# Slice by slice or tile by tile: the out-projection's end, its norm and the first FFN slice in another order

## The chip, the cores and the metric

The kernel runs on one core of a Trainium2 chip. The core has TensorE (PE in the rows; its weight loads are PEld), VectorE (DVE), ScalarE (ACT), GpSimd (POOL) and SyncE (SP), which issues nearly all loads. The metric is the device time of one execution, in microseconds (us), as the median of three runs.

## The reference, cut to what matters

The program is two transformer blocks in a row, 256 tokens by 1024 channels, in 32-bit floats. The first has attention and 32 experts. The second ends like this:

```python
mix = jnp.concatenate([attn, lru], axis=-1) @ w_out[l].astype(h.dtype)   # 1024 x 1024
x = x + rms_norm(mix, g_post_mix[l])
h = rms_norm(x, g_pre_ffn[l])
up = causal_dwconv(h @ w_up[l].astype(h.dtype), w_conv_ffn[l], b_conv_ffn[l])   # 1024 x 5632
c_u, c_g = jnp.split(up, 2, axis=-1)
ffn = (jax.nn.gelu(c_g, approximate=True) * c_u) @ w_down[l].astype(h.dtype)
x = x + rms_norm(ffn, g_post_ffn[l])
```

The change concerns the end of the product with `w_out`, the two norms behind it, and the first 256 columns of the product with `w_up`.

## The kernel before

**Split numbers.** A product keeps its precision by splitting both factors into an upper and a lower part, each of type fp32r, and adding three products: upper by upper, upper by lower, lower by upper (`mm3`). ScalarE writes the upper part as a rounded copy, VectorE the lower part as the difference. Weights are cut into slices of 128 x 2048 numbers, `s` counting them through the program. `split(s)` stands once in ScalarE's list (L768) and once in VectorE's (L1237). The parts go into `W`, which has two buffers, `s % 2`; `pair_free[s]` says when TensorE has read slice `s`, and `split(s)` on ScalarE waits for `pair_free[s - 2]`. The activations' parts are `X[:, 0]` and `X[:, 1]`, together `xin`.

**Order.** Each engine has its own list of instructions, written out by hand, and runs it in order; semaphores join them. The 256 tokens are two tiles `t` of 128. Weights come through a ring of eight places, loaded by SyncE in order; a place is loaded again once its slice is split (`lo_done`).

**Out-projection.** Slices 30 to 33 hold `w_out`, two blocks `k` of 128 rows each. For each `k`, tile and half `n` of the output columns, three matmuls over 512 columns add into a bank of PSUM `U_mix[t][n]`; so a slice is 24 matmuls. `rows_in` goes through slices 30, 31 and 32 with both tiles under each `k`. Only slice 33 goes tile by tile.

**Norms.** Of each finished half bank ScalarE takes the sum of squares (`square_rows`, L1152), then the root (`root_rows`, L786). VectorE multiplies by the gain (`gained`, L1857), takes the reciprocal (L1257) and adds to the residual `h` (`add_rows`, L1866). For the second norm ScalarE squares `h` (`square_h`, L1160) and takes the root; then the row is scaled into `u`: tile 0 by ScalarE (L1169), tile 1 by VectorE (L1885).

**Turns.** TensorE turns each tile, eight blocks of 128 x 128 (L2601), into banks `U_fT[t][0..1]`, four each. ScalarE rounds them with the gain into `X[:, 0]` (L1180), VectorE writes the remainder into `X[:, 1]` (L1896).

**FFN.** Slices 34 to 55 are `w_up`, 256 output columns each: 2 halves `m` x 8 `k` x 3 products = 48 matmuls, with the weights stationary and all 256 tokens moving. Slice 34 goes in `columns_first` (L2036): all upper by upper, then lower weights, then lower activations. The others go through `columns_in` (L1952). Slices 56 to 66 are `w_down`.

Of the kernel before, what the change touches and what calls it, by code (L numbers as in the profile page):

```python
# [8 lines left out]
F32 = mybir.dt.float32  # L9
# [7 lines left out]
P = 128  # L17
T = 256
# [96 lines left out]
def build_program(nc, I, out):  # L115
    ctx = ExitStack()
    with ctx:
        def sb(name, shape, dt=F32):
            return ctx.enter_context(nc.sbuf_tensor(name, shape, dt))

        def sem(name):
            return ctx.enter_context(nc.semaphore(name))
# [6 lines left out]
        h = sb("h", [P, 2, D])  # L129
        arena = sb("arena", [P, 20480])  # L130
# [267 lines left out]
        squares = Events(sem("s_squares"), attn=2, c=4, sb=2, mla=2, moe=2, ple=2, fin=4, mix=4, ffn=2, end=4)  # L398
        means = Events(sem("s_means"), fin=1)
        s_half = Events(sem("s_half_means"), mix=2, end=2)  # L400
        roots = Events(sem("s_roots"), attn=1, c=2, sb=1, mla=1, moe=2, ple=1, fin=2, mix=2, ffn=2, end=2)
        s_kT = sem("s_k_scaled")
        normed = Events(sem("s_normed"), attn=1, c=1, sb=1, mla=1, gates=1, fin=1, ffn=1)
# [32 lines left out]
        s_xfree, s_r0, s_u0 = sem("s_x_free"), sem("s_ffn_root0"), sem("s_ffn_rows0")  # L436
# [127 lines left out]

        def unloaded(n):
            if n in order:
                return lo_done(order[n])
            return BK.filled(U_pp[1][1]) if n == L_pp else used_at[n]
# [4 lines left out]
        def halved(s):  # L573
            n, b = SPL[s], s % 2
            w = loads[n][0]
            m = w.shape[1]
            return [W[:, b, j, 0:m * w.shape[2]].rearrange("p (a b) -> p a b", a=m) for j in range(2)]
# [177 lines left out]
        def _(e):  # L755
# [7 lines left out]
            def split(s):  # L763
                n = SPL[s]
                if s >= 2:
                    e.wait_ge(*pair_free[s - 2])
                e.wait_ge(s_land[loads[n][2]], 16 * loads[n][4])
                e.activation(halved(s)[0], loads[n][0], ACT.Copy).then_inc(s_hi, 1)  # L768
# [20 lines left out]
            def half_mean(name, t):  # L789
                e.wait_ge(*squares[name, 2 * t])  # L790
                e.activation(halfc[:, t:t + 1], ss[:, 2 * t:2 * t + 1], ACT.Identity, scale=1.0 / D,
                             bias=epsc).then_inc(s_half.sem, 1)

            def root_rows(name, t):
                e.wait_ge(*s_half[name, t])
                root(1, t, D, squares[name, 2 * t + 1], ss[:, 2 * t + 1:2 * t + 2], halfc[:, t:t + 1])
# [348 lines left out]
            split(33)  # L1145
            prime(ACT.Sqrt)
            split(34)
# [13 lines left out]

            square_rows("mix", 0, U_mix)
            root_rows("mix", 0)
            square_rows("mix", 1, U_mix)
            root_rows("mix", 1)
            square_h(0)
            root(1, 2, D, squares["ffn", 0], ss[:, 0:1])
            e.wait_ge(s_r0, 1)
            e.activation(u[:, 0, :], h[:, 0, :], ACT.Copy, scale=rs[:, 2:3]).then_inc(s_u0, 1)  # L1169
            square_h(1)  # L1170
            root(1, 3, D, squares["ffn", 1], ss[:, 1:2])

            for t in range(2):
                for i in range(2):
                    x = U_fT[t][i]
                    e.wait_ge(*BK.filled(x))
                    for j in range(4):
                        k = 4 * i + j
                        y = e.activation(X[:, 0, k, t * P:(t + 1) * P], ps[:, x[0], j * P:(j + 1) * P], ACT.Copy,  # L1180
                                         scale=col("g_pre_ffn_2", k))
                    y.then_inc(x_hi.sem, 1)
            split(35)
            prime(ACT.Gelu_apprx_tanh)
# [43 lines left out]
        def _(e):  # L1228
# [623 lines left out]
            split(33)  # L1852

            def gained(name, t, n, uses, gb):
                c = slice(n * 512, (n + 1) * 512)
                e.wait_ge(*squares[name, 2 * t + n])
                step(e.tensor_tensor(u[:, t, c], whole(uses[t][n]), gb[:, c], ALU.mult))  # L1857
# [13 lines left out]
            gained_rows("mix", 0, U_mix, gmix)  # L1871
            over_root("mix", 0, 0, 1)
            for n in range(2):
                add_rows(0, n, U_mix)
            gained_rows("mix", 1, U_mix, gmix)
            over_root("mix", 1, 1, 1)
            add_rows(1, 0, U_mix)
            e.wait_ge(*roots["ffn", 0])
            e.reciprocal(rs[:, 2:3], rs[:, 2:3]).then_inc(s_r0, 1)
            add_rows(1, 1, U_mix)  # L1880
            hi, lo = halved(34)
            e.wait_ge(s_hi, 35)
            e.tensor_tensor(lo[:, 0:4], loads[SPL[34]][0][:, 0:4], hi[:, 0:4].bitcast(F32), ALU.subtract)
            over_root("ffn", 1, 3, 1)
            e.tensor_scalar(u[:, 1, :], h[:, 1, :], rs[:, 3:4], None, ALU.mult).then_inc(normed.sem, 1)  # L1885
            e.tensor_tensor(lo[:, 4:8], loads[SPL[34]][0][:, 4:8], hi[:, 4:8].bitcast(F32), ALU.subtract).then_inc(s_lo, 1)

            for t in range(2):
# [46 lines left out]
            for t in range(2):  # L1936
                gained_rows("end", t, U_dd, gffn)
                over_root("end", t, t, 1)
                for n in range(2):
                    add_rows(t, n, U_dd)  # L1940
# [3 lines left out]
        def _(e):  # L1944
# [647 lines left out]
            for t in range(2):  # L2592
                if t == 0:
                    e.wait_ge(s_u0, 1)
                else:
                    e.wait_ge(*normed["ffn", 0])
# [6 lines left out]
            fT_ready = lambda k: [BK.emptied(U_fT[t][k // 4]) for t in range(2)]  # L2603
            fT_hi_ready = lambda k: [x_hi["ffn", 2 + k // 4]]
            for i in range(22):
                if i == 0:
                    columns_first(34, U_cv[0:2], range(KD), fT_hi_ready, fT_ready)
                    continue
# [55 lines left out]
```

## Time and profile before

| | us |
|---|---|
| median of 3 runs | 1410.53 |
| lowest, highest | 1408.81, 1411.22 |
| span of the profiled execution, first to last instruction | 1408.3 |
| its own total | not recorded apart from the span |
| TensorE busy in it | 1286.9 (91%) |
| TensorE's mean granted clock | 0.986 of full |

A profile is one execution; its times count from the first instruction. Busy times of several engines overlap, so shares don't add up to the span. A matmul's recorded duration includes its way through the array, which overlaps the next matmul: what one costs in a row is the distance from start to start. What ended a wait is inferred from semaphores. The granted clock is given as a share of 2.4 GHz: 1.00 is 2.4 GHz and 0.50 is 1.2 GHz.

### The profile page before, as it was taken

Reading aid. Unit: us, or ns where it says so; the run is one execution under the profiler, and the core shown is the slowest. Engines: PE = TensorE matmul, PEld = TensorE weight load, DVE = VectorE, ACT = ScalarE, POOL = GpSimd, SP = SyncE. Lnnn points to the kernel's source line nnn. Section 1 sums busy time; section 2 is a strip of 40 time slices with the busy share of each in tenths; the row PEclk is TensorE's granted clock in tenths of the full one; section 3 lists DMA queues with packets and bytes.
Section 4 is the critical chain, followed back from the end, with each engine's and each line's share of the span. In section 5 each row is a group of like instructions: output and inputs, shape, how many; then the busy total and the mean of one; then the engine's idle time right before and its main releaser. Section 6 shows DMA issues by size and latency. Waiting matters only on the chain.

```text
span 1408.3 us, 16583 instructions
## 1 busy us (share of the span) xinstructions
PE 1286.9 (91%) x6969; PEld 737.3 (52%) x6969; DVE 486.8 (35%) x730; ACT 401.2 (28%) x643; POOL 59.1 (4%) x115
## 2 busy tenths in 40 slices
PE   8999999999999889998888988889888999899998
PEld 7888433343333333333333332333324898799986
DVE  5895312112111111111211111111114687677765
ACT  5684212100110001100001000010004766655554
POOL 4001000000000000000000000000000510000000
PEclk9999899999999999999999999999999999899999
DMA  9548699999999999999999999999999964355520
GB/s 337 165 148 307 259 393 429 428 427 427 426 428 427 429 428 426 429 426 427 428 427 428 428 428 427 428 427 428 426 429 370 245 213 150 121 184 186 188 100 30
DMA packets 78474, 480.79 MB, mean 341 GB/s; under 512 B 5504, under 2 KB 40475, under 8 KB 53568
## 3 DMA queue, kind: packets, MB, share of 16 engines
q1 hardware_dynamic: 75904, 474.76, 83.3%
q0 software_dynamic: 2496, 4.96, 1.7%
q8 instruction: 57, 0.93, 0.3%
q14 instruction: 17, 0.14, 0.0%
HBM read 478.39 MB, written 1.31 MB: 341 GB/s over the span
## 4 chain that ended last, share of the span: by engine, by line
PE 52%; DMA 38%; DVE 4%; ACT 3%; issue 1%; DVEq 0%; ACTq 0%
DMA arena<-in_w_dn_dram 38%; PE ps L1952 22%; PE ps L2357 11%; PE ps L2397 11%; PE ps L2324 1%; PE ps L2413 1%; DVE W L1237 1%; PE ps L2036 1%; PE ps L1960 1%; PE ps L2514 1%; PE ps L2287 1%; ACT arena L960 0%; ACT arena L910 0%; PE ps L2368 0%; ACT W L768 0%
## 5 line engine op out<-in xcount | busy, mean ns | idle before, releaser
L2357 PE MATMUL ps<-ring,arena 128*64 128x512 f32 x1392 | 316.5, 597 | 12.0 <-DMA ring<-in_w_gu_dram 12.0
L2357 PEld LDWEIGHTS ps<-ring,arena 128*64 128x64 f32 x1392 | 97.4, 137 | 210.1 <-issue 179.1
L1952 PE MATMUL ps<-X,W 128*128 128x256 f32 x1560 | 191.4, 286 | 2.2 <-DVE W L1243 1.9
L1952 PEld LDWEIGHTS ps<-X,W 128*128 128x128 f32 x1560 | 190.2, 194 | 3.3 <-DVE W L1243 2.3
L1588 DVE TENSOR_SCALAR arena<-ps 128x512 f32<-128x512 f32 x32 | 22.1, 692 | 479.1 <-PE ps L2357 479.1
L1952 PE MATMUL ps<-W,X 128*128 128x512 f32 (+2 forms) x780 | 172.8, 380 | 2.7 <-issue 1.6
L1237 DVE TENSOR_TENSOR W<-ring,W 128x2048 fp32r<-128x2048 f32 (+2 forms) x64 | 144.9, 2264 | 78.9 <-ACT W L768 78.9
L2397 PE MATMUL ps<-ring,arena 128*64 128x512 f32 x648 | 145.7, 594 | 21.9 <-DMA ring<-in_w_dn_dram 21.9
L1952 PEld LDWEIGHTS ps<-W,X 128*128 128x128 f32 x780 | 141.5, 188 | 31.0 <-DVE W L1237 3.8
L973 ACT ACTIVATE arena<-arena 128x512 f32<-128x512 f32 x32 | 20.2, 630 | 460.2 <-DVE arena L1588 460.2
L2357 PE MATMUL ps<-arena 128*64 128x512 f32 x656 | 150.5, 599 | 0.0
L768 ACT ACTIVATE W<-ring 128x2048 fp32r<-128x2048 f32 (+2 forms) x65 | 122.6, 1887 | 81.5 <-PE ps L1952 80.5
L2397 PEld LDWEIGHTS ps<-ring,arena 128*64 128x64 f32 x648 | 48.4, 137 | 116.4 <-issue 115.8
L2397 PE MATMUL ps<-arena 128*64 128x512 f32 x376 | 85.8, 598 | 23.9 <-DMA arena<-in_w_dn_dram 23.9
L1616 DVE SCALAR_TENSOR_TENSOR X<-ps,arena,X 128x512 fp32r<-128x512 f32 x32 | 24.0, 751 | 219.7 <-ACT X L986 219.7
L986 ACT ACTIVATE X<-ps,arena 128x512 fp32r<-128x512 f32 x32 | 22.0, 687 | 258.4 <-PE ps L2397 258.4
L2357 PEld LDWEIGHTS ps<-arena 128*64 128x64 f32 x656 | 46.9, 138 | 91.1 <-issue 90.4
L2397 PEld LDWEIGHTS ps<-arena 128*64 128x64 f32 x376 | 25.1, 136 | 84.1 <-DMA arena<-in_w_dn_dram 42.4
L2324 PEld LDWEIGHTS ps<-X,W 128*128 128x128 f32 x256 | 33.7, 197 | 25.5 <-issue 24.9
L716 POOL CAST W<-arena 128x128 fp32r<-128x128 f32 x32 | 9.3, 293 | 871.0 <-PE ps L2357 851.4
L2413 PE MATMUL ps<-X,W 64*128 64x512 f32 x256 | 39.4, 425 | 6.5 <-DVE X L1616 6.5
L2368 PE MATMUL ps<-ident,arena 128*128 128x128 f32 x128 | 21.5, 291 | 25.6 <-ACT arena L960 25.6
(350 smaller groups left out, 991.4 us busy)
## 6 DMA issues: line engine op xcount, KB each, us to landing
ring<-in_w_gu_dram SPq DMA_DIRECT2D x87, 2048.0 KB, 22.4
ring<-in_w_dn_dram SPq DMA_DIRECT2D x40, 2048.0 KB, 24.5
arena<-in_w_gu_dram SPq DMA_DIRECT2D x39, 2048.0 KB, 20.4
arena<-in_w_dn_dram SPq DMA_DIRECT2D x23, 2048.0 KB, 25.6
ring<-in_w_up_dram SPq DMA_DIRECT2D x22, 1024.0 KB, 5.1
ring<-in_w_in_dram SPq DMA_DIRECT2D x15, 1024.0 KB, 12.6
ring<-in_w_down_dram SPq DMA_DIRECT2D x11, 1024.0 KB, 4.9
ring<-in_w_o_dram SPq DMA_DIRECT2D x4, 1024.0 KB, 4.9
```

What stands on the lines that cost most here:

```text
L768: e.activation(halved(s)[0], loads[n][0], ACT.Copy).then_inc(s_hi, 1)
L973: e.activation(sig, glu, ACT.Sigmoid, scale=1.702).then_inc(s_sig, 1)
L986: e.activation(yhi[x % 2], ps[:, DB, :], ACT.Copy, scale=gs[:, x:x + 1]).then_inc(s_yhi, 1)
L1237: e.tensor_tensor(lo, loads[SPL[s]][0], hi.bitcast(F32), ALU.subtract).then_inc(s_lo, 1)
L1588: e.tensor_scalar(glu, whole(gb), 7.0, None, ALU.min).then_inc(s_glu, 1)
L1616: e.scalar_tensor_tensor(out=ylo[x % 2], in0=ps[:, DB, :], scalar=gs[:, x:x + 1], in1=yhi[x % 2].bitcast(F32), op0=ALU.mult, op1=ALU.subtr ...
L1952: y = e.matmul(o, l, r, start=start and i == 0, stop=stop and i == 2)
L2324: y = e.matmul(ps[:, x[0], a * 256:(a + 1) * 256], part[:, t, k * P:(k + 1) * P], Sr[j % 2][:, t], start=part is uhi and t == 0, stop=part ...
L2357: y = e.matmul(ps[c * 64:c * 64 + 64, use[0], :], xs[:, k, c0:c0 + CAP], w[:, half * D + c * 512:half * D + (c + 1) * 512], start=False, s ...
L2368: y = e.transpose(ps[:, TB, j * P:(j + 1) * P], actv[:, j * P:(j + 1) * P], ident[:, :])
L2397: y = e.matmul(ps[c * 64:c * 64 + 64, DB, :], a, w[:, c * 512:(c + 1) * 512], start=kk == 0, stop=kk == KD - 1)
L2413: y = e.matmul(ps[:, b, :], GTr[x // 2 % 2][q, x % 2, t * P:(t + 1) * P], part[x % 2][q, :], start=x == 0 and part is yhi, stop=x == NE - ...
```

## The change

Six things are changed together.

1. Slices 32 and 33 are done by tile: 32 and 33 for tile 0, then both for tile 1 (`tile_rows`), 12 matmuls for each slice and tile.
2. The parts of slice 34 go into a third buffer, `arena_r`, laid over the arena's columns 11264 to 15359. The recurrent branch used these for `v2`, `xr`, `gr` and `xc`; the split waits until they have been read. From slice 35 on the buffers of `W` alternate with the other parity, and `split(35)` waits for slice 32, `split(36)` for slice 33. `split(34)` now stands directly behind `split(33)` on both engines.
3. The second norm of tile 0 is placed ahead of the first norm of tile 1, on both engines. VectorE scales both tiles.
4. Each tile is turned and rounded on its own.
5. Slice 34's product is done for each tile by itself, over 128 tokens: 48 matmuls for tile 0 behind its turns, then tile 1's turns, then 48 more.
6. Slice 35 does its two products with the upper weights first and the one with the lower weights last.

```diff
+        def pair_before(s):
+            return pair_free[{35: 32, 36: 33}.get(s, s - 2)]
...
         def halved(s):
-            n, b = SPL[s], s % 2
+            n, b = SPL[s], (s if s < 34 else s - 1) % 2
...
+            if s == 34:
+                return [arena_r[:, 11264 + 2048 * j:13312 + 2048 * j].rearrange("p (a b) -> p a b", a=m) for j in range(2)]
...
             def split(s):
                 n = SPL[s]
-                if s >= 2:
-                    e.wait_ge(*pair_free[s - 2])
+                if s == 34:
+                    e.wait_ge(s_lrul, 4)
+                    e.wait_ge(*BK.filled(U_o2[1]))
+                elif s >= 2:
+                    e.wait_ge(*pair_before(s))
...
             split(33)
+            split(34)
             prime(ACT.Sqrt)
-            split(34)
...
-            square_rows("mix", 0, U_mix)
-            root_rows("mix", 0)
-            square_rows("mix", 1, U_mix)
-            root_rows("mix", 1)
-            square_h(0)
-            root(1, 2, D, squares["ffn", 0], ss[:, 0:1])
-            e.wait_ge(s_r0, 1)
-            e.activation(u[:, 0, :], h[:, 0, :], ACT.Copy, scale=rs[:, 2:3]).then_inc(s_u0, 1)
-            square_h(1)
-            root(1, 3, D, squares["ffn", 1], ss[:, 1:2])
...
+            square_rows("mix", 0, U_mix)
+            root_rows("mix", 0)
+            square_h(0)
+            root(1, 2, D, squares["ffn0", 0], ss[:, 0:1])
+            square_rows("mix", 1, U_mix)
+            root_rows("mix", 1)
+            x_hi_rows(0)
+            square_h(1)
+            root(1, 3, D, squares["ffn1", 0], ss[:, 1:2])
             split(35)
+            x_hi_rows(1)
             prime(ACT.Gelu_apprx_tanh)
...
+            def normed_rows(t):
+                over_root(f"ffn{t}", 0, 2 + t, 1)
+                e.tensor_scalar(u[:, t, :], h[:, t, :], rs[:, 2 + t:3 + t], None, ALU.mult).then_inc(normed.sem, 1)
+
+            gained_rows("mix", 0, U_mix, gmix)
+            over_root("mix0", 0, 0, 1)
+            for n in range(2):
+                add_rows(0, n, U_mix)
+            normed_rows(0)
+            gained_rows("mix", 1, U_mix, gmix)
+            over_root("mix1", 0, 1, 1)
+            for n in range(2):
+                add_rows(1, n, U_mix)
+            x_lo_rows(0)
+            normed_rows(1)
+            x_lo_rows(1)
             split(35)
...
-            rows_in(32, (0, 1), 0, U_mix, xin, 4, 3, 512, 1024, mix_ready).then_inc(s_pair, 1)
-            rows_in(33, (2, 3), 0, U_mix, xin, 4, 3, 512, 1024, mix_ready, by_tile=True)
...
+            def tile_rows(s, ks, t, last):
+                hi, lo = halved(s)
+                e.wait_ge(*lo_done(s))
+                for n in range(2):
+                    use, c = U_mix[t][n], slice(n * 512, (n + 1) * 512)
+                    for i, k in enumerate(ks):
+                        e.wait_ge(*mix_ready(k))
+                        y = mm3(whole(use), [z[:, k, t * P:(t + 1) * P] for z in xin], (hi[:, i, c], lo[:, i, c]), False,
+                                last and k == ks[-1], True)
+                    if last:
+                        y.then_inc(full[use[0]], 1)
+                return y
+
+            tile_rows(32, (0, 1), 0, False)
+            tile_rows(33, (2, 3), 0, True)
+            tile_rows(32, (0, 1), 1, False).then_inc(s_pair, 1)
+            tile_rows(33, (2, 3), 1, True)
...
+            def tile_columns(s, t, uses):
+                hi, lo = halved(s)
+                e.wait_ge(s_hi, s + 1)
+                q = slice(t * P, (t + 1) * P)
+                for part, (w, z) in enumerate(((hi, xin[0]), (lo, xin[0]), (hi, xin[1]))):
+                    if part == 1:
+                        e.wait_ge(*lo_done(s))
+                    for m in range(2):
+                        c = slice(m * P, (m + 1) * P)
+                        if part == 0 and t == 0:
+                            claim(uses[m])
+                        for k in range(KD):
+                            if part == 0 and m == 0:
+                                e.wait_ge(*x_hi["ffn", 2 * t + k // 4])
+                            if part == 2 and m == 0:
+                                e.wait_ge(*BK.emptied(U_fT[t][k // 4]))
+                            y = e.matmul(ps[:, uses[m][0], q], w[:, k, c], z[:, k, q], start=part == 0 and k == 0,
+                                         stop=part == 2 and k == KD - 1)
+                        if part == 2 and t:
+                            y.then_inc(full[uses[m][0]], 1)
+
+            for t in range(2):
+                turned_tile(t)
+                tile_columns(34, t, U_cv[0:2])
```

## Rows read from the trace of the kernel before

**Rows 1.** The page, part 1: busy time, share of the span, instructions.

```profile
PE 1286.9 (91%) x6969; PEld 737.3 (52%) x6969; DVE 486.8 (35%) x730; ACT 401.2 (28%) x643; POOL 59.1 (4%) x115
```

**Rows 2.** The chain of waits, 1186 to 1222: start, duration, what.

```profile
1187.02 16.38 PE ps L1952 x72
...
1207.15 1.14 ACT arena L1160 x2
...
1208.84 0.76 DVE arena L1885
...
1210.80 1.15 ACT X L1180 x4
...
1212.09 8.68 PE ps L2036 x48
```

**Rows 3.** Timeline of TensorE: start, duration, instructions, in brackets the idle time before.

```profile
1207.30 1.52 PE L2601 MATMUL ps<-ident,arena 128*128 128x128 f32 x8 [3.91 <-ACT arena L1169]
1209.65 1.97 PE L2601 MATMUL ps<-ident,arena 128*128 128x128 f32 x8 [0.83 <-DVE arena L1885]
...
1220.60 24.64 PE L1952 MATMUL ps<-X,W 128*128 128x256 f32 x204
```

**Rows 4.** Timeline of ScalarE.

```profile
1192.55 1.92 ACT L768 ACTIVATE W<-ring 128x2048 fp32r<-128x2048 f32 x1 [3.47 <-PE ps L1952]
...
1200.71 0.60 ACT L1152 ACTIVATE arena<-ps 128x512 f32<-128x512 f32 x1
...
1204.20 0.29 ACT L786 ACTIVATE sm<-sm 128x1 f32<-128x1 f32 x1
...
1208.52 4.46 ACT L1180 ACTIVATE X<-ps,cols 128x128 fp32r<-128x128 f32 x16
```

**Rows 5.** Timeline of VectorE.

```profile
1194.49 2.29 DVE L1237 TENSOR_TENSOR W<-ring,W 128x2048 fp32r<-128x2048 f32 x1 [2.87 <-ACT W L768]
...
1202.22 1.42 DVE L1866 SCALAR_TENSOR_TENSOR h<-arena,sm,h 128x512 f32<-128x512 f32 x2
...
1210.64 4.22 DVE L1896 SCALAR_TENSOR_TENSOR X<-ps,cols,X 128x128 fp32r<-128x128 f32 x16
```

**Rows 6.** Short matmuls: timeline of TensorE, one line's durations, groups by shape.

```profile
171.11 0.95 PE L2383 MATMUL ps<-sm,msk 128*128 128x1 f32 x8
...
304.20 1.71 PE L2383 MATMUL ps<-sm,msk 128*128 128x1 f32 x8
...
L2383 PE MATMUL ps<-sm,msk x128: 169/250/352, 171.1 to 1010.4; 128*128 128x1 f32 x128
...
L2563 PE MATMUL ps<-arena 128*128 128x256 f32 x16 | 3.6, 379 | 0.0
...
L2552 PE MATMUL ps<-arena,sm 128*128 128x128 f32 x4 | 0.6, 273 | 0.0
```

**Rows 7.** Windows: length, busy times (instructions), granted clock, DMA share, GB/s.

```profile
core 0: us, PE busy (x) PEld busy (x) DVE busy (x) ACT busy (x) POOL busy (x), PEclk, DMA share, GB/s
1078.10:1081.50 3.40, 3.02 (x15) 3.05 (x16) 3.40 (x4) 2.63 (x7) 0.00 (x0) 0.50 1.05 383
1081.60:1083.00 1.40, 1.40 (x9) 1.18 (x8) 1.40 (x4) 1.40 (x5) 0.00 (x0) 1.00 1.08 371
1175.20:1180.40 5.20, 5.20 (x50) 5.20 (x48) 5.05 (x13) 3.67 (x6) 0.00 (x0) 1.00 0.42 146
146.30:149.60 3.30, 3.29 (x15) 3.30 (x16) 2.52 (x5) 0.84 (x2) 0.00 (x0) 0.50 0.09 37
1212.10:1218.00 5.90, 5.90 (x27) 5.86 (x28) 5.00 (x12) 4.16 (x7) 0.00 (x0) 0.50 0.50 173
1220.60:1385.00 164.40, 163.44 (x1197) 156.00 (x1196) 120.02 (x159) 89.96 (x116) 0.00 (x0) 1.00 0.45 150
```

**Rows 8.** Timeline of TensorE in earlier stages at a low clock.

```profile
1076.56 1.21 PE L2413 MATMUL ps<-X,W 64*128 64x512 f32 x8 [1.57 <-DVE X L1616]
...
1078.48 3.41 PE L1960 MATMUL ps<-ident,h 128*128 128x128 f32 x16 [0.71 <-DVE h L1697]
...
139.16 3.34 PE L2300 MATMUL ps<-wr,arena 128*128 128x32 f32 x16 [0.58 <-ACT arena L946]
```

More of the change, by code:

```diff
@@ L129, in build_program @@
         h = sb("h", [P, 2, D])
+        with nc.sbuf_tensor("arena_r", [P, 20480], F32R) as arena_r:
+            pass
         arena = sb("arena", [P, 20480])
@@ L397, in build_program @@
         pool = Events(sem("s_pool"), zero=1, ident=1, mzero=2, msk=3, iota=1, one=1, tri=2, i32=1, ez=1, eoh=2, wz=1)
-        squares = Events(sem("s_squares"), attn=2, c=4, sb=2, mla=2, moe=2, ple=2, fin=4, mix=4, ffn=2, end=4)
+        squares = Events(sem("s_squares"), attn=2, c=4, sb=2, mla=2, moe=2, ple=2, fin=4, mix0=2, ffn0=1, mix1=2, ffn1=1, end0=2, end1=2)
         means = Events(sem("s_means"), fin=1)
-        s_half = Events(sem("s_half_means"), mix=2, end=2)
-        roots = Events(sem("s_roots"), attn=1, c=2, sb=1, mla=1, moe=2, ple=1, fin=2, mix=2, ffn=2, end=2)
+        s_half = Events(sem("s_half_means"), mix0=1, mix1=1, end0=1, end1=1)
+        roots = Events(sem("s_roots"), attn=1, c=2, sb=1, mla=1, moe=2, ple=1, fin=2, mix0=1, ffn0=1, mix1=1, ffn1=1, end0=1, end1=1)
         s_kT = sem("s_k_scaled")
-        normed = Events(sem("s_normed"), attn=1, c=1, sb=1, mla=1, gates=1, fin=1, ffn=1)
+        normed = Events(sem("s_normed"), attn=1, c=1, sb=1, mla=1, gates=1, fin=1, ffn=2)
         x_hi = Events(sem("s_x_hi"), attn=4, c=3, sb=2, mla=2, ple=4, fin=2, fin2=2, lru=4, aT=2, ffn=4)
@@ L435, in build_program @@
         lru = Events(sem("s_lru_pool"), ix=1, av2=1, it=1)
-        s_xfree, s_r0, s_u0 = sem("s_x_free"), sem("s_ffn_root0"), sem("s_ffn_rows0")
+        s_xfree = sem("s_x_free")
         s_lru, s_lrul = sem("s_lru"), sem("s_lru_lo")
@@ L789, in half_mean @@
             def half_mean(name, t):
-                e.wait_ge(*squares[name, 2 * t])
+                e.wait_ge(*squares[f"{name}{t}", 0])
                 e.activation(halfc[:, t:t + 1], ss[:, 2 * t:2 * t + 1], ACT.Identity, scale=1.0 / D,
@@ L794, in root_rows @@
             def root_rows(name, t):
-                e.wait_ge(*s_half[name, t])
-                root(1, t, D, squares[name, 2 * t + 1], ss[:, 2 * t + 1:2 * t + 2], halfc[:, t:t + 1])
+                e.wait_ge(*s_half[f"{name}{t}", 0])
+                root(1, t, D, squares[f"{name}{t}", 1], ss[:, 2 * t + 1:2 * t + 2], halfc[:, t:t + 1])
             e.wait_ge(*pool["one", 0])
@@ L1160, in square_h, with x_hi_rows @@
                 e.activation(u[:, t, :], h[:, t, :], ACT.Square, accum_out=ss[:, t:t + 1]).then_inc(squares.sem, 1)
-            square_rows("mix", 0, U_mix)
-            root_rows("mix", 0)
-            square_rows("mix", 1, U_mix)
-            root_rows("mix", 1)
-            square_h(0)
-            root(1, 2, D, squares["ffn", 0], ss[:, 0:1])
-            e.wait_ge(s_r0, 1)
-            e.activation(u[:, 0, :], h[:, 0, :], ACT.Copy, scale=rs[:, 2:3]).then_inc(s_u0, 1)
-            square_h(1)
-            root(1, 3, D, squares["ffn", 1], ss[:, 1:2])
-            for t in range(2):
+            def x_hi_rows(t):
                 for i in range(2):
@@ L1852, in _ @@
             split(33)
+            split(34)
             def gained(name, t, n, uses, gb):
                 c = slice(n * 512, (n + 1) * 512)
-                e.wait_ge(*squares[name, 2 * t + n])
+                e.wait_ge(*squares[f"{name}{t}", n])
                 step(e.tensor_tensor(u[:, t, c], whole(uses[t][n]), gb[:, c], ALU.mult))
@@ L1870, in _, with x_lo_rows @@
             e.wait_ge(s_gmix, 16)
[L1871 to L1889, printed above, removed]
+            def x_lo_rows(t):
                 for i in range(2):
@@ L1937, in _ @@
                 gained_rows("end", t, U_dd, gffn)
-                over_root("end", t, t, 1)
+                over_root(f"end{t}", 0, t, 1)
                 for n in range(2):
@@ L2587, in _, with turned_tile @@
             rows_in(31, (6, 7), 0, U_mix, xin, 4, 3, 512, 1024, mix_ready).then_inc(s_pair, 1)
-            rows_in(32, (0, 1), 0, U_mix, xin, 4, 3, 512, 1024, mix_ready).then_inc(s_pair, 1)
-            rows_in(33, (2, 3), 0, U_mix, xin, 4, 3, 512, 1024, mix_ready, by_tile=True)
[L2592 to L2596, printed above, removed]
+            def tile_rows(s, ks, t, last):
[14 more added lines that the diff above has]
+            tile_rows(33, (2, 3), 1, True)
+            def turned_tile(t):
+                e.wait_ge(*normed["ffn", t])
                 for i in range(2):
@@ L2602, in _ @@
                     y.then_inc(full[x[0]], 1)
[L2603 to L2607, printed above, removed]
+            def tile_columns(s, t, uses):
[21 more added lines that the diff above has]
+                tile_columns(34, t, U_cv[0:2])
+            for i in range(1, 22):
+                if i == 1:
+                    hi, lo = halved(35)
+                    e.wait_ge(s_hi, 36)
+                    for m in range(2):
+                        x, c = U_cv[2 + m], slice(m * P, (m + 1) * P)
+                        claim(x)
+                        for part, (w, z) in enumerate(((hi, xin[0]), (hi, xin[1]), (lo, xin[0]))):
+                            if part == 2 and m == 0:
+                                e.wait_ge(*lo_done(35))
+                            for k in range(KD):
+                                y = e.matmul(whole(x, T), w[:, k, c], z[:, k, :], start=part == 0 and k == 0,
+                                             stop=part == 2 and k == KD - 1)
+                        y.then_inc(full[x[0]], 1)
                     continue
```

## The prediction

> **What bounds the kernel now.** The page's table of engines comes first: TensorE is busy 91% of the span [rows 1]. The place of the change is found in the chain of waits: up to 1203.40 us the chain is TensorE alone (72 matmuls of the last three out-projection slices, 16.38 us, 0.2275 each), then for 8.7 us it runs through ScalarE and VectorE (squares, root, scaling, turns, rounding), and at 1212.09 it returns to TensorE [rows 2]. The timeline of TensorE gives the two idle stretches, 3.91 and 0.83 us, and the start of FFN slice 35 at 1220.60 [rows 3]. From there to 1385 TensorE is busy 163.44 of 164.40 us [rows 7], so the start of slice 35 is what counts: a shift there arrives at the end in full. The timelines of ScalarE and VectorE [rows 4, 5] price what the new order arranges. The windows [rows 7] show the last thing to read: behind the gap the granted clock was 0.50 (1.2 of 2.4 GHz) up to 1218.0, 27 matmuls of slice 34 in 5.9 us, 0.213 to 0.219 each, where the 204 from 1220.60 on take 24.64 us, 0.120 each [rows 3]. From 1203.40 to 1220.60 the kernel thus spends 17.2 us on a slice that needs 48 x 0.120 = 5.8: 8.7 of it is the gap, 2.7 the slow clock.
>
> **What stays.** Slice 31 ends at 1203.40 - 48 x 0.2275 = 1192.48, as before. The weights of slice 33 go into the buffer that slice 31 has read, so their split still begins at 1192.55 on ScalarE and ends on VectorE at 1194.49 + 2.29 = 1196.78 [rows 4, 5].
>
> **Out-projection by tile.** Tile 0 now wants slice 33 after 12 matmuls of slice 32, at 1192.48 + 2.73 = 1195.21, where before it wanted it after 24. TensorE waits 1.6 us for the lower half. It then needs 0.17 us to fill and 12 x 0.2275: tile 0 is complete at 1199.73, 0.94 us sooner than before (1200.67), and tile 1 after 24 more at 1205.19, 1.79 us later than 1203.40. The split of slice 34 goes into the third buffer directly behind 33's on both engines (1.92 us on ScalarE, 2.29 on VectorE to 1199.1), ahead of tile 0's squares at 1199.76. What hides it is TensorE's own work on slices 32 and 33; put behind the first square it would cost its 1.92 us. The two half splits that VectorE did among tile 1's steps are gone. Its buffer lies over the recurrent branch's tiles, whose last readers are done before slice 31 begins at 1187.02 [rows 2]. The load whose slot this split frees is issued some 11 us sooner; nothing waits for it.
>
> **Tile 0's norm.** Before, from the second square's start (1200.71) to the end of the two additions (1202.22 + 1.42 = 1203.64) it took 2.93 us [rows 4, 5]; now 1199.76 + 2.93 = 1202.69. From square_h to the first turn it took 1207.15 to 1209.65, 2.50 us [rows 2, 3]: now 1202.75 to 1205.25. TensorE leaves the out-projection at 1205.19, so this gap is closed. Tile 0's scaling moves from ScalarE to VectorE (0.76 us there, as tile 1's had [rows 2]), ahead of tile 1's products, which wait for tile 1's first square (near 1205) anyway.
>
> **Tile 0's columns.** Eight turns, 0.11 each, begin at 1205.25; the first four fill the first bank at 1205.85. ScalarE is then with tile 1's squares and root, which took 1203.42 to 1204.49 before [rows 2, 4] and now end at 1205.22 + 1.07 = 1206.29; behind them wait the roundings, 16 in 4.46 us, so 1.12 for each bank [rows 4]: ready at 1207.4 and 1208.55. TensorE starts four matmuls at 1207.5 and the other 44 at 1208.65. VectorE ends tile 1's additions at 1205.22 + 2.93 = 1208.15 and its eight remainders (4.22/16 = 0.264 each [rows 5]) at 1210.3, before part 2 wants them.
>
> **The price of a 128-column matmul** decides. Slice 34's 48 matmuls over 256 columns become 96 over 128. With split weights none stands in the trace. What a row of n takes from one to the next is its time less the last one's duration, over n - 1. A 128-column weight load with one column moved behind it goes at (0.95 - 0.17)/7 = 0.111 us; unsplit numbers over 128 columns at (0.6 - 0.27)/3 = 0.11 [rows 6]. The bounds lie further out: below, half of 0.120, 0.060; above, 0.215, the unsplit 256-column matmul ((3.6 - 0.38)/15). I take 0.109, since both rows agree and each matmul here has its own weight load. So a tile costs nearly what both together cost: 96 x 0.109 = 10.5 us against 5.8.
>
 At the low level the row says (1.71 - 0.25)/7 = 0.209 us [rows 6], twice the rule. By the rule a low clock would cost these matmuls nothing; by the row it doubles them, and I go by the row (0.213, as for 256 columns).
>
> **The sum at full clock.** Tile 0: 1208.65 + 44 x 0.109 = 1213.45. Tile 1's norm is hidden behind it: square_h(1) at 1208.55, scaled by VectorE at about 1211.25. But TensorE turns it only behind tile 0's columns, 1213.45 to 1214.35; ScalarE, free since its split of slice 35 at 1211.95, rounds by 1215.2 and 1216.35; four matmuls run at 1215.3 and 44 from 1216.45, to 1221.25. Slice 35 starts 0.65 us later than at 1220.60. Its lower weights are there at 1216.35 + 1.1 + 2.3 = 1219.75, wanted at about 1223. So at full clock the 8.7 + 2.7 = 11.4 us go, and 12.1 come in their place: 1.8 of slice 33's wait, 4.7 of weight loads, 1.8 of turns, 3.8 of waits for the two roundings (1.4 + 0.7 and 1.0 + 0.7): +0.7 us.
>
> **The clock.** Before, it fell behind 3.9 us idle, but also behind less: 1.57 us idle, a burst of 1.21 us and 0.71 idle, with 0.50 granted from 1078.1 [rows 7, 8]. The new order has two such stretches: 1205.2 to 1208.65 (turns of 0.9 us and four matmuls in it) and 1213.45 to 1216.45 (the same), each with half-filled matmuls behind. In 1175.2 to 1180.4, 64-column matmuls paced by weight loads kept the clock at 1.00, so such matmuls alone don't lower it. Do they raise it? Sixteen turns did so between 1078.1 and 1081.6; sixteen 32-column matmuls from 139.16 didn't, and it was at 0.50 to 149.6, the last 3.3 us of it dense. The split columns lie between the two. I take them with the latter: fp32r streams 256 columns in 0.120 where unsplit numbers need 0.215, so a split matmul of 128 moves half of what a turn moves behind the same weight load.
>
> If it falls with the first stretch, say at 1209.3, four microseconds behind the last out-projection matmul: 39 of tile 0's matmuls pay 0.104 more (4.1), the turns 0.4, tile 1's 44 pay 4.6, and slice 35 runs slow until the clock is back, 3.3 us (146.3 to 149.6) to 5.9 (1212.1 to 1218.0) at 0.213 for 0.120, 2.0 us: 0.7 + 4.1 + 0.4 + 4.6 + 2.0 = +11.8. If it falls with the second, about as late in it, at 1217.7: 33 x 0.104 = 3.4, + 2.0 + 0.7 = +6.1. Which of them can't be told; the middle is +9.0. The profiled span is 1408.3, its own total isn't given apart; the median of the runs is 1410.53, 2.2 us above, and I add to the median: 1419.5.
>
> **Rivals.**
> Clock kept, or back soon. For it: the 5.2 us at 1.00 on weight-paced matmuls, and the turns that raised it. It gives +0.7 (1411.2), or, where some 16 matmuls run slow, 1.7 more (1412.9), or, where a low clock cost these columns nothing, slice 35's 2.0 alone (1413.2), against which stands the 0.209 of the row; the skill's rule on weight loads above is this last case. Against it: two thin stretches in a row, of which either suffices.
> Faster. The mechanism is the weight load hidden by its neighbour, so that 128 columns take 0.060 us. Then tile 0's columns end at 1208.65 + 44 x 0.060 = 1211.3, the turns at 1212.3, the roundings at 1213.2 and 1214.35, the columns at 1214.45 + 2.7 = 1217.15: -3.4, 1407.1. From a price under about 0.10 us on the change is ahead at full clock, under 0.07 measurably. The skill's page (Back-to-back issue gap) has 81 ns for sustained 128-column pairs, by which the sum would be +0.7 - 88 x 0.028 = -1.8; no row shows it. Against it: both rows at 0.11.
> Dearer columns. At 0.215 the 88 exposed matmuls add 9.3 us at full clock (+10.0, 1420.5), and more with a low one, beyond 1422.5. For it there is only that no split matmul under 256 columns is in the trace.
>
> **How the numbers follow.** Low clock that stays until slice 35: 0.48, own range 1416.6 to 1422.3, forecast 1419.5. Clock kept 0.19, back soon 0.09, low at no cost 0.02. Faster 0.13. Dearer 0.09. Within 0.2% (2.8 us), the measurement tells nothing: those are these three, 0.30; faster 0.13; slower 0.48 + 0.09 = 0.57. The range 1408.5 to 1422.5 leaves out the faster case and the worst of the dear one.
>
> **What would show it.** TensorE: a wait of 1.6 us before slice 33; no wait longer than 0.3 before tile 0's first turn; waits of about 1.2 and 0.5 us around the first four column matmuls, 0.9 and 0.5 for tile 1; 0.109 us from one column matmul to the next at 1.00, 0.21 at 0.50; slice 35's start near 1221.3 at full clock, near 1230 with the clock low since tile 0, the clock at 1.00 again some microseconds behind. I am wrong if the columns go at 0.06, if nothing waits at slice 33, or if the clock stays at 1.00 throughout.

## The result and the profile after

| | median, us | lowest to highest | executions |
|---|---|---|---|
| before | 1410.3 | 1408.81 to 1411.22 | 6 |
| changed | 1417.14 | 1414.68 to 1422.16 | 6 |

The change makes the kernel slower: the ratio is 1.0059, with a 95% interval from 1.0048 to 1.0070. The median moved by 6.8 us; 9.0 were forecast, within 6.1 to 11.8. The spread moved too: 2.4 us before, 7.5 us after. The profiled execution is the fastest of the six, with a span of 1413.0 us.

The timeline of TensorE in the changed kernel, answering to [rows 3] (start, duration, instructions, idle time before):

```profile
1185.99 8.45 PE L1961 MATMUL ps<-W,X 128*128 128x512 f32 x36
1196.05 8.46 PE L1961 MATMUL ps<-W,X 128*128 128x512 f32 x36 [1.61 <-DVE W L1246]
1204.65 1.09 PE L2622 MATMUL ps<-ident,arena 128*128 128x128 f32 x8
1206.92 0.63 PE L2641 MATMUL ps<-X,arena_r 128*128 128x128 f32 x4 [1.17 <-DVE h L1876]
1207.74 5.13 PE L2641 MATMUL ps<-X,arena_r 128*128 128x128 f32 x44 [0.19 <-ACT X L1178]
1212.71 1.06 PE L2622 MATMUL ps<-ident,arena 128*128 128x128 f32 x8
1214.66 0.63 PE L2641 MATMUL ps<-X,arena_r 128*128 128x128 f32 x4 [0.89 <-ACT X L1178]
1215.60 7.72 PE L2641 MATMUL ps<-X,arena_r 128*128 128x128 f32 x44 [0.31 <-ACT X L1178]
1223.12 8.10 PE L2660 MATMUL ps<-X,W 128*128 128x256 f32 x48
```

This execution reached slice 31's end 0.75 us sooner than the one before, so distances count. The first two rows have slice 33's wait, 1.61 us. Tile 0's turns follow the out-projection without a gap: the 3.91 us of [rows 3] are gone. The two waits around the first four columns are there for each tile, 1.17 and 0.19, then 0.89 and 0.31. Three of them end with ScalarE's roundings. The first is put down to an addition on VectorE (L1876): tile 0's columns are written into a bank that tile 1's addition frees, which the forecast does not name. It costs 0.1 us at most: from a tile's first rounding to its first column it is 1.39 us here (1205.53 to 1206.92) and 1.29 for tile 1 (1213.37 to 1214.66), and the other 44 columns wait for the roundings in any case. The rows of 44 show the price: tile 0's take 5.13 us, (5.13 - 0.28)/43 = 0.113 each, and tile 1's 7.72. Slice 35 (L2660) needs 8.10 us for its 48, where 5.8 is the price at full clock. The windows say why (length, busy times, granted clock):

```profile
core 0: us, PE busy (x) PEld busy (x) DVE busy (x) ACT busy (x) POOL busy (x), PEclk, DMA share, GB/s
1204.60:1217.60 13.00, 10.39 (x86) 9.69 (x86) 8.72 (x24) 9.80 (x25) 0.00 (x0) 1.00 0.00 1
1217.80:1227.90 10.10, 10.10 (x49) 10.10 (x48) 5.24 (x6) 2.82 (x3) 0.00 (x0) 0.50 0.36 112
1228.00:1385.00 157.00, 156.04 (x1153) 149.43 (x1153) 113.92 (x153) 84.92 (x111) 0.00 (x0) 1.00 0.47 154
```

The granted clock fell to 0.50 at about 1217.7, in tile 1's columns, and was back near 1228. So the profiled execution is the forecast's second case, a fall with tile 1's stretch. From slice 31's end (1191.73) to slice 35's start (1223.12) are 31.4 us, where the sum at full clock had 1221.25 - 1192.48 = 28.8: the 2.6 between them are some 26 columns at 0.21 in place of 0.11.

The chain of waits of the changed kernel, where [rows 2] had ScalarE and VectorE for 8.7 us:

```profile
1189.90 1.83 PE ps L1961 x8
...
1196.05 8.47 PE ps L1961 x36
...
1204.55 0.70 ACT arena L1162 x2
...
1205.62 2.08 ACT X L1178 x8
...
1207.74 5.13 PE ps L2641 x44
...
1213.37 2.19 ACT X L1178 x8
...
1215.60 7.72 PE ps L2641 x44
```

Behind the out-projection it leaves TensorE twice, first for ScalarE's last square, root and roundings of tile 0, then for the roundings of tile 1; the columns can't start without them.

### The profile page after: what moved, and what is told of

Read it like the earlier page. It is cut to its first block, busy times and chain, and to the rows that moved or that the text cites. A ratio compares the mean times of both kernels' runs of the same rounds, so it can differ in the third digit from the quotient of the medians.

```text
span 1413.0 us, 16673 instructions
## 1 busy us (share of the span) xinstructions
PE 1292.0 (91%) x7017; PEld 741.4 (52%) x7017; DVE 487.6 (35%) x730; ACT 399.9 (28%) x642; POOL 59.0 (4%) x115
## 4 chain that ended last, share of the span: by engine, by line
PE 49%; DMA 40%; DVE 5%; ACT 4%; issue 1%; DVEq 0%; ACTq 0%
DMA arena<-in_w_dn_dram 38%; PE ps L1961 21%; PE ps L2406 11%; PE ps L2366 10%; DMA ring<-in_w_dn_dram 2%; DVE W L1246 1%; PE ps L2333 1%; PE ps L2641 1%; PE ps L2422 1%; ACT W L778 1%; PE ps L2523 1%; PE ps L2660 1%; ACT arena L920 0%; PE ps L2296 0%; ACT arena L970 0%
## 5 line engine op out<-in xcount | busy, mean ns | idle before, releaser
L1961 PE MATMUL ps<-X,W 128*128 128x256 f32 x1512 | 185.5, 286 | 2.2 <-DVE W L1252 2.0
L1961 PEld LDWEIGHTS ps<-X,W 128*128 128x128 f32 x1512 | 184.4, 194 | 3.3 <-DVE W L1252 2.4
L2333 PEld LDWEIGHTS ps<-X,W 128*128 128x128 f32 x256 | 33.7, 197 | 25.5 <-issue 24.9
```

The lines of the kernel that those rows point to most:

```text
L1961: y = e.matmul(o, l, r, start=start and i == 0, stop=stop and i == 2)
L2333: y = e.matmul(ps[:, x[0], a * 256:(a + 1) * 256], part[:, t, k * P:(k + 1) * P], Sr[j % 2][:, t], start=part is uhi and t == 0, stop=part ...
```

## The experiments

Each kernel was timed beside the kernel before on the same chip. Those of one group below shared a chip.

### First group: one part undone, or one cost taken out

**pair_columns**: the change with slice 34 again over 256 columns.

```diff
             for t in range(2):
                 turned_tile(t)
-                tile_columns(34, t, U_cv[0:2])
+            columns_first(34, U_cv[0:2], range(KD), lambda k: [x_hi["ffn", 2 + k // 4]],
+                          lambda k: [BK.emptied(U_fT[t][k // 4]) for t in range(2)])
```

> The changed kernel, but slice 34's product again over both tiles' 256 columns, behind both turns (48 matmuls, not 96). My theory (the loss is the weight loads of twice as many matmuls, and the clock, which these don't raise): TensorE starts the product near 1213.3, at a low clock behind some 5 us of idle time, 8.5 us for 48, so slice 35 starts about 1.1 us later than in the kernel before: 1411.5, and the runs lie within 3 us of each other. Rival (the new order of the norms and of the splits on ScalarE and VectorE costs the time): it stays near 1417.

Measured: 1412.07 (1410.34 to 1413.52), ratio 1.0011 [1.0002, 1.0019]. Of the loss of 6.8 us all but 2 are gone, although the norms and the splits kept their new order. The rival falls. The gap that the change closed is open again, 4.72 us, and yet it is faster. The clock falls here too, from about 1210.2 to 1220.5, but it is back before slice 35 starts:

```profile
1206.19 1.09 PE L2622 MATMUL ps<-ident,arena 128*128 128x128 f32 x8
1212.00 1.97 PE L2622 MATMUL ps<-ident,arena 128*128 128x128 f32 x8 [4.72 <-DVE arena L1895]
1214.43 8.71 PE L2045 MATMUL ps<-X,arena_r 128*128 128x256 f32 x48 [0.47 <-ACT X L1178]
```

**filled_waits**: the change, with matmuls that nobody reads in TensorE's waits. They do no work of the reference.

```diff
+            def filler(n):
+                e.wait_ge(s_hi, 35)
+                claim(U_cv[2])
+                for _ in range(n):
+                    e.matmul(whole(U_cv[2]), arena_r[:, 11264:11392], arena_r[:, 11264:11776], start=True, stop=True)
...
                             if part == 0 and m == 0:
+                                if k == 4:
+                                    filler(2)
                                 e.wait_ge(*x_hi["ffn", 2 * t + k // 4])
...
                 turned_tile(t)
+                filler(4)
                 tile_columns(34, t, U_cv[0:2])
```

> The changed kernel with idle TensorE time filled by matmuls over 512 columns into a bank that nobody reads: 4 behind each tile's turns, 2 behind the first four column matmuls of each tile. My theory: the granted clock stays at 1.00, the rest goes on as planned, 0.7 us over the kernel before: 1411 (at most 1412), and the spread of 7.5 us between runs shrinks to that of the kernel before. Rival (the clock is a side effect): 1417 as the change, or above it by the added work.

Measured: 1411.33 (1410.09 to 1413.81, 12 executions), ratio 1.0010 [1.0001, 1.0018]. Adding twelve matmuls of 0.23 us brings the changed kernel from 6.8 to 1.2 us over the kernel before. Its windows:

```profile
1197.50:1222.00 24.50, 24.11 (x160) 21.05 (x160) 15.99 (x33) 15.69 (x41) 0.00 (x0) 1.00 0.28 89
1222.00:1240.00 18.00, 18.00 (x152) 18.00 (x151) 13.79 (x19) 9.53 (x12) 0.00 (x0) 1.00 0.56 180
```

The clock is 1.00 throughout, and what is left over the kernel before, 1.2 us, is near the 0.7 of the sum at full clock. So the low clock was some 5.6 of the 6.8 us. This doesn't add to what pair_columns took away: the split columns cost time of their own and also left the clock low.

**third_for_33**: the third buffer for slice 33, and slice 34 in slice 31's.

```diff
-            return pair_free[{35: 32, 36: 33}.get(s, s - 2)]
+            return pair_free[{34: 31, 35: 32}.get(s, s - 2)]
...
-            n, b = SPL[s], (s if s < 34 else s - 1) % 2
+            n, b = SPL[s], (s if s < 33 else s - 1) % 2
...
-            if s == 34:
+            if s == 33:
                 return [arena_r[:, 11264 + 2048 * j:13312 + 2048 * j].rearrange("p (a b) -> p a b", a=m) for j in range(2)]
...
-                if s == 34:
+                if s == 33:
                     e.wait_ge(s_lrul, 4)
```

> The changed kernel, but the third buffer holds slice 33, and slice 34 goes into the buffer that slice 31 has left. My theory: slice 33's parts are ready near 1194, TensorE no longer waits 1.6 us for them, everything behind is 1.7 us earlier and otherwise the same: 1415.4, with the same wide spread. Rival (the wait is hidden behind ScalarE's chain, which sets the roundings): no change, 1417.

Measured: 1420.24 (1417.71 to 1421.23, 6 executions), 1.0064 [1.0051, 1.0077]. Both expectations miss. The wait is gone, but everything behind it got slower:

```profile
1188.96 8.45 PE L1961 MATMUL ps<-W,X 128*128 128x512 f32 x36
1197.25 2.88 PE L1961 MATMUL ps<-arena_r,X 128*128 128x512 f32 x12
...
1205.71 1.09 PE L2622 MATMUL ps<-ident,arena 128*128 128x128 f32 x8
1207.98 0.63 PE L2641 MATMUL ps<-X,W 128*128 128x128 f32 x4 [1.17 <-DVE h L1876]
1208.79 8.42 PE L2641 MATMUL ps<-X,W 128*128 128x128 f32 x44 [0.18 <-ACT X L1178]
1217.01 1.93 PE L2622 MATMUL ps<-ident,arena 128*128 128x128 f32 x8
1219.41 10.59 PE L2641 MATMUL ps<-X,W 128*128 128x128 f32 x48 [0.47 <-ACT X L1178]
```

```profile
1205.70:1210.10 4.40, 3.03 (x24) 2.69 (x24) 4.29 (x12) 4.28 (x15) 0.00 (x0) 1.00 0.00 0
1210.30:1234.00 23.70, 23.23 (x109) 22.82 (x109) 8.48 (x16) 8.20 (x14) 0.00 (x0) 0.50 0.14 45
1234.10:1240.00 5.90, 5.90 (x51) 5.90 (x50) 2.38 (x6) 2.88 (x4) 0.00 (x0) 1.00 0.54 179
```

Here is the forecast's first case: the fall comes 4.5 us behind tile 0's turns, and for 23.9 us the clock stays at 0.50, although TensorE is recorded as busy for 23.23 of the window's 23.70 us. A reader who looks only at the busy share sees a full engine. In these 23.9 us run some 80 split columns, eight turns and then some 20 of slice 35's matmuls over 256 columns (1229.79 to 1234.0), with which the clock comes back.

**before_filled**: the kernel before with filler in its idle stretches, 16, 3 and 1.

```diff
+            filler(16)
             for t in range(2):
                 if t == 0:
                     e.wait_ge(s_u0, 1)
...
                     y.then_inc(full[x[0]], 1)
+                filler(3 if t == 0 else 1)
```

> The kernel before, with its idle stretches filled by 16, 3 and 1 matmuls over 512 columns into a bank that nobody reads. My theory: the granted clock stays at 1.00 through slice 34, whose 48 matmuls take 5.9 us and not 8.5: 2.6 us faster than before, 1407.7. Rival (the low clock costs little, since something else is late by then): within 0.5 us of before.

Measured: 1408.35 (1406.05 to 1411.98), 0.9989 [0.9979, 0.9999]: 1.7 us off the median where 2.6 were expected. The interval, 0.1 to 3.0 us, holds both 2.6 and the rival's 0.5, so the median alone doesn't decide between them. The profile does: it has slice 34's matmuls at full clock, and slice 35 starts 2.4 us sooner, counted from slice 31's start:

```profile
1186.11 16.61 PE L1952 MATMUL ps<-W,X 128*128 128x512 f32 x72
1202.55 3.79 PE L2596 MATMUL ps<-W 128*128 128x512 f32 x16
...
1212.13 5.54 PE L2036 MATMUL ps<-X,W 128*128 128x256 f32 x44 [0.23 <-ACT X L1180]
1217.51 27.76 PE L1952 MATMUL ps<-X,W 128*128 128x256 f32 x230
```

This run is also the like for filled_waits, on the same chip and with the clock held in both: 1411.33 against 1408.35. At full clock the new order is 3.0 us slower than the old.

### Second group: the rest without the clock, and a better order

**third33_filled**: third_for_33 with the filler of filled_waits.

> Slice 33 in the third buffer, and the waits filled as in filled_waits, so that the clock stays up. The third_for_33 run came out slower than the change, not faster, and its profile has the clock at 0.50 from 1210.2 to 1234; this run takes the clock out. My theory (slice 33's wait costs 1.7 us in full, and third_for_33 met the early fall of the clock in its runs): 1.7 us under filled_waits, 1409.6, the range of the kernel before. Rival (the wait at slice 33 is hidden, or the other place of the buffers costs something of its own): 1411.3 as filled_waits, or above.

Measured: 1409.59 (1408.0 to 1411.31), 0.9998 [0.9989, 1.0007]. With the clock held, the other place of the buffer saves 1.7 us against filled_waits, though the two medians are from two chips; in the profiles it is 1.9. Slice 33's wait is a real cost, paid in full. With neither wait nor low clock, the new order is as fast as the kernel before, but that kernel still pays for its own low clock. Against before_filled, which doesn't, it is some 1.2 us slower.

**buffer_alone**: the kernel before, with slice 34 in the third buffer and its split directly behind slice 33's on both engines, nothing else.

```diff
             split(33)
+            split(34)
             prime(ACT.Sqrt)
-            split(34)
...
-            e.tensor_tensor(lo[:, 0:4], loads[SPL[34]][0][:, 0:4], hi[:, 0:4].bitcast(F32), ALU.subtract)
...
-            e.tensor_tensor(lo[:, 4:8], loads[SPL[34]][0][:, 4:8], hi[:, 4:8].bitcast(F32), ALU.subtract).then_inc(s_lo, 1)
```

> The kernel before with the third buffer alone: slice 34's parts in it, its split directly behind slice 33's on both engines, the two half splits on VectorE gone; order of TensorE, norms and columns as before. My theory: the buffer costs nothing and frees little, 0 to 0.5 us faster than before. Rival (the loss of the change lies in the earlier split or in the buffer's place): 2 us or more slower.

Measured: 1409.86, 0.9997 [0.9988, 1.0006]. The buffer and the earlier split cost nothing, and alone they bring nothing that can be measured.

**pair_best**: slice 33 in the third buffer, slice 34 over 256 columns, slice 35's split behind tile 1's roundings, filler.

```diff
-            split(35)
             x_hi_rows(1)
+            split(35)
...
             for t in range(2):
                 turned_tile(t)
-                tile_columns(34, t, U_cv[0:2])
+                filler((20, 4)[t])
+            columns_first(34, U_cv[0:2], range(KD), lambda k: [x_hi["ffn", 2 + k // 4]],
+                          lambda k: [BK.emptied(U_fT[t][k // 4]) for t in range(2)])
```

> Slice 33 in the third buffer, slice 34 over both tiles' 256 columns, split of slice 35 behind tile 1's roundings, and 20 and 4 matmuls over 512 columns as filler behind the two tiles' turns. My theory: the out-projection ends as in the kernel before, tile 1's turns start 5.9 us behind it, the 48 column matmuls 1.8 us later at full clock: slice 35 starts 3.5 us sooner than in the kernel before, 1406.6. Rival (the tile-wise columns are needed to gain anything): no better than before_filled, 1408.4.

Measured: 1406.6 (1405.59 to 1408.72), 0.9978 [0.9968, 0.9988]. It is 3.3 us faster than the kernel before beside it. Whether it is faster than before_filled isn't clear: the ratios, 0.9978 and 0.9989, differ by 1.6 us, but their intervals overlap, and in the profiles slice 35 starts 0.5 us sooner.

```profile
1203.29 1.09 PE L2622 MATMUL ps<-ident,arena 128*128 128x128 f32 x8
1204.13 4.82 PE L2628 MATMUL ps<-arena_r 128*128 128x512 f32 x20
1209.09 1.09 PE L2622 MATMUL ps<-ident,arena 128*128 128x128 f32 x8
...
1212.01 5.54 PE L2045 MATMUL ps<-X,W 128*128 128x256 f32 x44 [0.23 <-ACT X L1178]
1217.39 5.92 PE L2667 MATMUL ps<-X,W 128*128 128x256 f32 x48
```

**change_again**: the changed kernel once more.

> The changed kernel itself once more, as a second profile and for its spread beside the others of this call. My theory: the clock falls behind tile 0's turns or behind tile 1's, by execution, so its runs form two groups some 5 us apart: near 1415 to 1416 with a fall in the second stretch, near 1420 to 1422 with one in the first; mean granted clocks near 0.988 and 0.983. Rival (a fixed price): runs within 3 us of each other, as the kernel before has them.

Measured: 1416.15 (1414.14 to 1419.5, 5 executions), 1.0050 [1.0036, 1.0063]. With the first six there are eleven executions. Three have a mean granted clock of 0.983 and take 1419.5, 1421.32 and 1422.16. The other eight have 0.986 to 0.990 and take 1414.14 to 1418.16. So by the clock there are two sorts of execution; by the times alone there is no gap between them, since 1418.16 lies nearer to 1419.5 than to the next below it, 1416.76. Its profile again has the fall in tile 1's columns, at about 1217.3. That the three had the fall behind tile 0 is inferred from their clocks and times, since neither profile of this kernel shows it.

### Third group: each stretch by itself

**first_filled** and **second_filled**: filled_waits with the filler around one tile's roundings only.

```diff
-                filler(4)
+                filler(4 if t == 0 else 0)
...
-                                    filler(2)
+                                    filler(2 if t == 0 else 0)
```

> The changed kernel with filler matmuls (4 and 2) only around tile 0's roundings, none around tile 1's. My theory (each thin stretch can bring its own fall): no fall behind tile 0, so the runs near 1420 to 1422 vanish, the highest stays under 1418.5; falls behind tile 1 remain in most executions: median 1415 to 1416. Rival (one stretch, tile 0's, is the trigger of all): 1411.5 as filled_waits.

Measured: 1415.26 (1411.29 to 1415.84, 6 executions), 1.0027 [1.0013, 1.0041]. Nothing above 1416 is left. One execution, 1411.29 us with a mean clock of 0.994, is as fast as filled_waits. The profile has no fall behind tile 0 and one at about 1217.1, in tile 1's columns, whose 44 take 8.89 us.

> The changed kernel with filler matmuls (4 and 2) only around tile 1's roundings, none around tile 0's. My theory: where the clock falls behind tile 0 it stays low to the end of slice 34 and the run takes 1420 to 1422, plus a little for the filler at a low clock; where it doesn't, 1411 to 1412. Two groups with nothing between, in shares that go by execution. Rival (filler near the end brings the clock back): all near 1412 to 1415.

Measured: 1412.81 (1409.29 to 1416.91, 12 executions), 1.0021 [1.0008, 1.0034]. Here I was wrong. The times don't form two groups, and none reaches 1420. The rival's mechanism fits better, though the times spread beyond its 1412 to 1415. The profile met the fall behind tile 0, up to which this kernel is the changed one unaltered, and shows why it is cheap here:

```profile
1203.00:1207.10 4.10, 2.72 (x21) 2.37 (x21) 3.99 (x11) 4.01 (x13) 0.00 (x0) 1.00 0.01 2
1207.20:1217.30 10.10, 10.10 (x48) 9.91 (x47) 1.92 (x7) 3.57 (x9) 0.00 (x0) 0.50 0.00 0
1217.50:1223.00 5.50, 5.50 (x48) 5.33 (x46) 3.79 (x8) 2.07 (x5) 0.00 (x0) 1.00 0.11 20
```

The clock is back at about 1217.3, behind tile 1's eight turns (from 1214.64) and during the four filler matmuls (1216.22 to 1217.9), where in third_for_33 and third_again it stayed low through the same turns, a wait, and 48 more split columns. So filler may not only hold the clock but bring it back; one profile against two of another kernel is what there is for it.

**pair_unfilled**: pair_best without filler.

> pair_best without its 24 filler matmuls. It measured 1406.6 with them. My theory: the same start of slice 34 near 1211.1, but at 0.50 for some 6 us of its 8.5: 2.6 us more, 1409.2. Rival (the order alone brings the gain): 1406.6.

Measured: 1409.22 (1408.46 to 1411.01), 0.9994 [0.9984, 1.0003]. The 24 matmuls without use are worth 2.3 us by the ratios and 2.6 by the medians; the order alone about 0.9, not clear of zero.

**third_again**: third_for_33 once more.

> third_for_33 once more: the change with slice 33 in the third buffer, no filler. All six of its runs had a mean granted clock of 0.981 to 0.984 and took 1417.7 to 1421.2. If it was chance that all met the fall behind tile 0, some runs now have 0.988 or more and take about 1413 to 1415. Rival: without the wait at slice 33 the fall behind tile 0 is certain, and all runs again have 0.984 or less and 1417.5 or more.

Measured: 1421.01 (1419.61 to 1422.03, 5 executions), 1.0073 [1.0059, 1.0087], mean granted clocks 0.980 to 0.984. The rival holds: by their clocks and times eleven of eleven executions of this kernel meet the fall behind tile 0, against three of eleven for the change. In both profiles it came 4.0 to 4.5 us behind the start of tile 0's turns (1210.2, with turns at 1205.71 and 1206.20).

### The profiles beside the medians

For the runs whose clock is back before slice 35, the table sets the profile beside the median. The columns: the starts of slice 31 and of slice 35 in the profile, the distance between them, what it differs from the kernel before, and what the median differs from that of the kernel before beside it.

| | slice 31 | slice 35 | distance, us | profile | median |
|---|---|---|---|---|---|
| before | 1186.78 | 1220.60 | 33.82 | | |
| before_filled | 1186.11 | 1217.51 | 31.40 | -2.4 | -1.7 |
| buffer_alone | 1185.15 | 1218.46 | 33.31 | -0.5 | -0.1 |
| pair_columns | 1187.53 | 1222.99 | 35.46 | +1.6 | +2.0 |
| filled_waits | 1187.45 | 1222.07 | 34.62 | +0.8 | +1.2 |
| third33_filled | 1189.03 | 1221.74 | 32.71 | -1.1 | -0.4 |
| pair_best | 1186.53 | 1217.39 | 30.86 | -3.0 | -3.3 |
| pair_unfilled | 1187.27 | 1220.08 | 32.81 | -1.0 | -1.1 |

## Why it came as forecast, and what was off

**Slice 33's wait.** 1.6 us were worked out, 1.61 stand in the profile, and third33_filled against filled_waits shows that they count in full (1.7).

**Tile 0's norm and the closed gap.** Forecast: no wait over 0.3 us ahead of the turns. The timeline has none. This is what the change does for its price.

**The columns.** The price of a 128-column matmul was the term on which the sign hung. 0.109 was taken between bounds of 0.060 and 0.215; measured are 0.113 in the changed kernel at full clock. The faster and the dearer rival fall with it. The sum at full clock, +0.7 us, was tested by filled_waits: +1.2, with an interval of 0.1 to 2.5 us, and +0.8 in its profile. The same sum has 2.7 us of slow clock on the side of the kernel before; without them it says +3.4, and filled_waits against before_filled is +3.0.

**The waits for roundings.** 1.2 and 0.5 were forecast, then 0.9 and 0.5; 1.17 and 0.19, then 0.89 and 0.31 are recorded as idle. The second of each pair is shorter because the second bank was rounded sooner than reckoned: the 44 columns start 3.09 and 2.89 us behind the start of their tile's turns, where 3.40 and 3.00 were forecast. What this saved, 0.4 us, 88 columns at 0.113 instead of 0.109 took back.

**The clock.** That it falls behind one of the two thin stretches, and that the split columns don't bring it back, was argued from likeness to two rows. third_for_33 shows both: 23.9 us at 0.50 with TensorE recorded as busy. filled_waits shows what the clock is worth, by taking it out. The price of the two cases was forecast as +6.1 (1416.6) and +11.8 (1422.3); the two sorts of execution of the changed kernel lie at 1414.1 to 1418.2 and 1419.5 to 1422.2. By the medians of these two sorts they cost +5.8 and +11.0. Two small slips lie in these sums: eight turns at the low clock cost 8 x 0.104 = 0.8 us and not 0.4 (1.93 against 1.09 us in third_for_33), and tile 0's end, 1199.73, is 0.05 more than its terms give. Split columns go at 0.11 us with the clock at 1.00; at 0.50 tile 1's 48 in third_for_33 go at (1229.79 - 1219.41)/48 = 0.22, any short wait included. The Trainium skill (TensorE: Matmul & The Clock Gate, LDWEIGHTS) puts a weight load at columns/1.2 ns and names no clock in it; by that alone a low clock would have cost the columns nothing, and these figures speak against it, as the forecast's row did.

**What was off.** The forecast stood in the middle between the two cases, with the open question which is more frequent. Of the six executions of the result four took the cheaper one, of all eleven eight, and so the median is 2.4 us under 1419.5. The mechanism was right, and the share of the cases was mis-sized. How near the median came to 9.0 is luck: it depends on the mix of two cases, which the forecast couldn't tell. Of the 0.30 for a clock that stays, comes back soon or costs nothing, nothing was seen: none of the eleven executions is at 1411 to 1413.

**Where the expected gain went.** The change hides an idle time of 3.9 us behind useful work. But the useful work costs nearly twice as much in the small pieces that fit: 96 matmuls of 0.11 us for 48 of 0.12. Doing tile 0's half in the gap saves nothing of what remains, since tile 1's half then takes almost as long as both tiles together. third33_filled has the change at its best: it is as fast as the kernel before with that kernel's slow clock left in, and some 1.2 us slower than before_filled, where both have full clock.

**What stays open.** What decides which stretch the fall follows wasn't found. With 1.6 us of waiting taken out ahead of it, all eleven executions had the dear case. But that edit also moved slice 34's parts from the third buffer into `W`, and change_again, third_for_33 and third_again ran on three different chips, so neither the wait nor the stretch's place in the execution is shown to be the cause; no run moved the stretch by small steps. And before_filled gained 1.7 us where its profile has 2.4, which its interval, 0.1 to 3.0 us, allows.

## What to carry to other kernels

Before an idle stretch is filled with work cut in half, price the halves: here a matmul over 128 columns cost what a weight load with one column behind it cost (0.113 and 0.111 us), and two halves cost nearly twice the whole. Compare like with like: a kernel whose waits are filled belongs beside the kernel before with its waits filled too. Where the idle time can't be used, matmuls without use over 512 columns are worth their place, since they held the clock for what follows: 24 of them gave 2.3 to 2.6 us here. Read the granted clock beside the busy share, and the spread of the runs beside their median: one that triples tells of something that only some executions meet.

## What the runs showed of the hardware

A TensorE that is recorded as busy isn't one that keeps its clock: in third_for_33 it was busy for 23.23 of 23.70 us, and the granted clock was 0.50 throughout. In it ran some 80 matmuls over 128 fp32r columns, each behind a weight load of 128, eight turns, and some 20 matmuls over 256 columns, with which the clock rose at 1234.0.

Where the clock falls differed between two kernels: by their mean clocks and times, 11 of 11 executions of third_for_33 met the fall behind tile 0, and 3 of 11 of the change. The two kernels differ by a wait of 1.6 us ahead of it and by the buffers of slices 33 and 34; which of these matters isn't shown.

In second_filled the clock rose at about 1217.3 us, during four matmuls over 512 columns behind eight turns, with split columns before and after them.
